# Where the sums of squares are formed: GpSimd or VectorE, and when TensorE takes them up

## The chip, the cores and the metric

The kernel runs on one core of a Trainium2 chip. The metric is the time on the device in microseconds. Three runs of the kernel before gave 1308.89, 1309.41 and 1309.84 us, median 1309.41.

## The reference

Two decoder layers work on a stream x of 512 tokens by 1024 features, all in f32. Layer 0 mixes tokens by an RWKV-7 recurrence, layer 1 by dilated attention; both also attend to 256 memory tokens, and both end in a gated MLP with a causal convolution of width 3. The change is about three of the RMS norms:

```python
def rmsnorm(x, g):
    xf = f32(x)
    return xf * lax.rsqrt(jnp.mean(xf * xf, axis=-1, keepdims=True) + RMS_EPS) * f32(g)
# layer i:  h = rmsnorm(x, attn_norm[i]); ... x = x + y @ w_out
#           x = x + conv_ffn(x, ...)   where conv_ffn starts with rmsnorm(x, g) @ w_up
```

## The kernel before, in words

The stream is kept with features on the 128 partitions: x is eight slices (KD = 8) of 128 by 512 tokens. Every matrix product is made of three products of rounded parts: a weight tile is split into w_hi, a copy that ScalarE rounds, and w_lo, the difference that VectorE forms (L2118) or GpSimd (L3036); the stream's slices likewise into in_hi and in_lo, or b_hi and b_lo. Weight tiles come by DMA into a ring of four slots. w_hi and w_lo have two buffers, so ScalarE can round tile n once TensorE is through with tile n-2.

Each engine runs a program written out by hand, in order; semaphores tie them together. A norm is not applied before the product. TensorE multiplies the raw stream; meanwhile the sum over the features of x squared is formed, and the result of the product is scaled when VectorE reads it (L2548). For the sum, ScalarE squares each slice of x into y (L1793 before an MLP, L1843 for layer 1), GpSimd adds the slices y[1] to y[6] to y[0], one after the other, each add waiting for the one before it (sum_squares, L3008, L3014), and TensorE multiplies by a matrix of ones.

The four places of the change:

1. MLP start (square_sum, L1161, called in mlp ahead of the second of the first two up-projection tiles). TensorE makes two products of ones, with y[0], the sum, and with y[7], into bank 7. The rows of the trace call them "bank<-y,cst 128x512"; each f32 product is two passes. Then ScalarE takes the root (stream_root, L1515), VectorE the reciprocal (stream_rstd, L2111), and VectorE reads the first tile's product. In VectorE's order the low part of the fourth tile stands behind that read and the one after it, and in ScalarE's order the high part of the fourth tile behind own_tap of the first. A tile is eight k-steps of three matmuls (split_product, L675).

2. The down-projection of the first MLP's second half runs in four rounds o, each of two slices of x. The weights of a round come as seven blocks (A11, A12, A22, S2, S4, S1, S3), each rounded by ScalarE (block_high) and VectorE (block_low). Behind its blocks of a round ScalarE does stream_high(m), which makes b_hi[m] and y[m] from the finished slice m of x: m = 2o after the next round's A22, and m = 2o + 1 at the end of the round. GpSimd adds the squares as they come.

3. Layer 1's projections, 20 tiles s. In tile s TensorE runs over four groups r of tokens and two k-steps b, and at slot 2r + b it calls between(s, slot). token_sums (L1247) is called at tile 1, slot 4: products of y[0] and y[7] with two columns of ones ("bank<-cst,y 128x2"), which give the sums by token. VectorE's order here: stream_low(0) to (7), that is b_lo, then rope_tables, then in tile 1 token_rms (L2662), which waits for the sums. GpSimd forms w_lo of tile s + 2.

4. Second MLP: residual (L2399) on VectorE and squares (L1784) on ScalarE go through the eight slices of x; GpSimd adds; square_sum as in 1.

Of the kernel before, what the change touches and what calls it, by code (L numbers as in the profile page):

```python
# [145 lines left out]
def trunk(nc, xT, memT, consts, params, ropes, masks, w_small, w_mem, w_pairs, w_ring, outT):  # L146
    ctx = ExitStack()
    with ctx:
# [242 lines left out]
        def part_count(stage, o, i):  # L391

            if o == 0:
                at = 1 if i is None else i + 2
            else:
                at = 5 if i is None else 6 if i == S4 else i + 1
            return 2 * PAIRS + 1 + 6 * (4 * stage + o) + at

        def parts_used(stage, o, i):
            return 3 * (N_OUTA + 3 * PAIRS) + 7 * (4 * stage + o) + i + 1  # L400
# [262 lines left out]
        def _(pe):  # L663
# [496 lines left out]

            def square_sum(q):  # L1161

                pe.wait_ge(sem("sq_sum"), (KD - 2) * (q + 1))
                mm(bank[7][:, :], ones, y[:, 0, :], True, False)
                pe.wait_ge(sem("xsq"), KD * (q + 2))
                mm(bank[7][:, :], ones, y[:, KD - 1, :], False, True).then_inc(sem("x_ss"), 1)

            def mlp(l, h_at):
                for half in range(2):
                    up, down = mlp_tiles(l, half)  # L1170
                    g0 = FT * l + HALF * half
                    e, stage = 3 * l + 1 + half, 2 * l + half

                    def up_pair(p, q, j):
                        if not isinstance(p, int) or g0 + p >= 2:
                            pe.wait_ge(sem("up_read"), 2 * p + 2 * (g0 - 1))
                        for s in range(2):
                            if half == 0 and q == 0 and s == 1:
                                square_sum(2 * l)
                            if half == 1 and q == 0 and s == 1:  # L1180
                                pe.wait_ge(sem("x_up"), KD * e)
                            n = up + 2 * q + s
                            split_ready(2 * p + (up + s))
                            b = 2 * ((g0 + q) % 2) + s
                            split_product(bank[b][:, :], n, in_hi, in_lo, KD,
                                          ready=("h_ready", h_at + 1) if q == 0 and s == 0 and half == 0 else None)\
                                .then_inc(used, 1)

                    mlp_pairs(pe, up_pair)

                    def product(o, i, out, adds=False):

                        part = MOVING[i]
                        if i < S1:
                            pe.wait_ge(sem("part_lo"), part_count(stage, o, i))
                        else:
                            split_ready(down + 2 * o + i - S1)
                        hi, lo = block_slot(w_hi_all, o, i), block_slot(w_lo_all, o, i)
                        for j in range(ZP):
                            ks = slice(j * P, (j + 1) * P)  # L1200
                            at = slice(PARTW * j + TH * part, PARTW * j + TH * (part + 1))
                            mm(out, hi[:, ks], z[:, 0, at], j == 0 and not adds, False)
                            mm(out, hi[:, ks], z[:, 1, at], False, False)
                            q = mm(out, lo[:, ks], z[:, 0, at], False, j == ZP - 1)
                        return q

                    def plain(o, s, ks=range(ZC)):

                        out = bank[down_banks(g0, o)[s]][:, :]
                        pe.wait_ge(sem("part_lo"), part_count(stage, o, None))  # L1210
                        for k in ks:
                            p = (0, HALF - 2, HALF - 1)[k]
                            if o == 0:
                                pe.wait_ge(sem("z"), z_count(stage, p))
                            cs = slice(k * P, (k + 1) * P)
                            first = k == 0 and o == 0
                            mm(out, plain_slot(w_hi_all)[:, s, cs], z_plain(0, p), first, False)
                            mm(out, plain_slot(w_hi_all)[:, s, cs], z_plain(1, p), False, False)
                            q = mm(out, plain_slot(w_lo_all)[:, s, cs], z_plain(0, p), False, k == ZC - 1)
                        return q  # L1220

                    pe.wait_ge(sem("z"), z_count(stage, 2, ZP - 1, 2))
                    for o in range(4):
                        a, b, c = (bank[i] for i in down_banks(g0, o))
                        low, high = slice(0, TH), slice(TH, T)
                        pe.wait_ge(sem("x_up"), KD * e + 2 * (o - 1) if o > 1 else KD * e)
                        if o == 1:
                            pe.wait_ge(sem("up_read"), 2 * (g0 + HALF))
                        if o == 0:
                            plain(o, 0, (0, 1))  # L1230
                            plain(o, 1, (0,))
                        product(o, A11, c[:, low]).then_inc(sem("part_used"), 1)
                        product(o, A12, a[:, low], o == 0).then_inc(sem("part_used"), 1)
                        product(o, A22, b[:, low], o == 0).then_inc(sem("part_used"), 1)
                        pe.wait_ge(sem("accumulated"), added(stage, o, 1))
                        product(o, S2, c[:, low], True).then_inc(sem("part_used"), 1)
                        product(o, S4, a[:, high], True).then_inc(sem("part_used"), 1)
                        plain(o, 0, range(2 if o == 0 else 0, ZC)).then_inc(used, 1)
                        pe.wait_ge(sem("accumulated"), added(stage, o, 2))
                        product(o, S1, c[:, low]).then_inc(sem("part_used"), 1)  # L1240
                        plain(o, 1, range(1 if o == 0 else 0, ZC)).then_inc(sem("part_used"), 1)
                        pe.wait_ge(sem("x_up"), KD * e + 2 * o + 1)
                        product(o, S3, c[:, low]).then_inc(used, 1)
# [2 lines left out]

            def token_sums():  # L1247

                pe.wait_ge(sem("sq_sum"), 2 * (KD - 2))
                pe.wait_ge(sem("xsq"), 3 * KD)  # L1250
                for r in range(RES):
                    for m in (0, KD - 1):
                        q = mm(bank[7][:, 2 * r:2 * r + 2], residues(y[:, m, :])[:, r, :], ones[:, 0:2], m == 0, m > 0)
                q.then_inc(sem("x_ss"), 1)
# [74 lines left out]

            def between(s, slot):  # L1330

                if (s, slot) == (1, 4):
                    token_sums()
                if slot == 1 and 5 <= s <= 16:
                    turn_heads(s - 5)
# [123 lines left out]
        def _(act):  # L1459
# [343 lines left out]
            def mlp(l):  # L1803
                for half in range(2):
# [86 lines left out]
                    for o in range(4):  # L1891
                        if o:
                            block_high(o, S4)
                        block_high(o, S1)
                        block_high(o, S3)
                        if o < 3:
                            block_high(o + 1, A11)
                            block_high(o + 1, A12)
                            block_high(o + 1, A22)
                            stream_high(2 * o)  # L1900
                            block_high(o + 1, S2)
                            plain_high(o + 1)
                            stream_high(2 * o + 1)
                    split(down + KD)
                    stream_high(KD - 2)
                    split(down + KD + 1)
# [11 lines left out]
                copy(w_hi[:, n % 2, 0:w], ring[:, i, 0:w]).then_inc(sem("w_hi"), 1)  # L1918

            mlp(0)  # L1920
            act.wait_ge(sem("sq_sum"), 2 * (KD - 2))

            def group_done(g, r):

# [78 lines left out]
            for s in range(GROUPS * PARTS + 1):  # L2003
# [2 lines left out]
                    squares_out(g - 1, RES - 1)  # L2006
                if 0 < s < GROUPS * PARTS:
                    split(N_PROJ + s + 1)
                if s == 1:
                    act.wait_ge(sem("x_eps"), 2)  # L2010
                    root(tok_rstd, bank[7][:, 0:8], D, rms_eps).then_inc(sem("x_sd"), 1)
                if s in KV_AT:
# [89 lines left out]
        def _(dve):  # L2102
# [698 lines left out]
            def operand_low(i):  # L2801
# [2 lines left out]
                dve.wait_ge(sem("in_hi"), 5 * KD + 1 + i + 1)  # L2804
                lower(out_b_operand(k)[1], y[:, k, :], out_b_operand(k)[0], "y_split")

            rope_tables()
            for s in range(GROUPS * PARTS):
                g = s // PARTS
                if s == 1:  # L2810
                    token_rms()
                if s in (3, 7, 11):
                    rope_parts(g, 0)
# [88 lines left out]
            operand_low(2)  # L2902
            operand_low(3)
            residual(N_OUTB, 3, 0.5)
            mlp(1, 0)


        @block.gpsimd
        def _(pool):
# [95 lines left out]
                pool.wait_ge(sem("q_high"), Q0 + 12 * PAIRS + i + 1)  # L3005
                G.tensor_tensor(out_low[k], y[:, k, :], out_high[k].bitcast(F32), ALU.subtract).then_inc(sem("y_split"), 1)

            def sum_squares(q):  # L3008

                for m in range(1, KD - 1):  # L3010
                    pool.wait_ge(sem("xsq"), KD * (q + 1) + m + 1)
                    if m > 1:
                        pool.wait_ge(sem("sq_sum"), (KD - 2) * q + m - 1)
                    G.tensor_tensor(y[:, 0, :], y[:, 0, :], y[:, m, :], ALU.add).then_inc(sem("sq_sum"), 1)  # L3014

            sum_squares(0)
            sum_squares(1)
            pool.wait_ge(sem("w_lo"), N_PROJ + 2 - N_SPLIT)
            def head_scaled(e):

# [20 lines left out]
                    for e in range(2 * s - 18, 2 * s - 16):  # L3041
                        head_scaled(e)

            sum_squares(2)

# [124 lines left out]
```

## Time and profile before

| what | value |
|---|---|
| median of three runs | 1309.41 us |
| profiled execution | 1308.9 us |
| its span | 1307.0 us |
| TensorE busy | 1275.2 us, 98% |
| VectorE busy | 992.2 us, 76% |
| ScalarE busy | 646.0 us, 49% |
| GpSimd busy | 321.3 us, 25% |
| granted TensorE clock, mean | 1.000 |

The span is the time from the first to the last instruction of the profiled execution; the execution's own time is 1.9 us longer. Busy shares are of the span. A row of a timeline gives the start from the beginning of the span, the length, engine, line and operation, the tiles written and read, the shape, and in brackets for how long the engine sat idle before it and what released it. Neighbouring instructions of one kind are merged into one row with their count.

### The profile page before, as it was taken

The page shows a single profiled execution, that of the slowest core. Times are in us where ns is not written, and L with a number is a line of the kernel's source. Part 1 is how long each engine was busy: PE and PEld are TensorE (multiplying, and loading weights), DVE is VectorE, ACT ScalarE, POOL GpSimd, SP SyncE. Part 2 cuts the span into 40 slices and gives each one's busy share as a digit, 9 for nine tenths or more (in the row PEclk, how much of TensorE's full clock was granted, in tenths as well). Part 3 has the DMA queues.
Part 4 walks back from the last instruction along what each step waited for, and adds up shares of the span by engine and source line. Part 5 has one row for each costly group of instructions (what it writes and reads, how often), then busy time and mean ns, then how long its engine had stood idle before and what let it go on. Part 6 is the DMA issues. An engine that isn't in the chain of part 4 may idle for free.

```text
span 1307.0 us, 27113 instructions
## 1 busy us (share of the span) xinstructions
PE 1275.2 (98%) x10688; PEld 1041.3 (80%) x10688; DVE 992.2 (76%) x1486; ACT 646.0 (49%) x1068; POOL 321.3 (25%) x302
## 2 busy tenths in 40 slices
PE   7999999999999999999999999999999999999999
PEld 5876777776578888988889988776778889888898
DVE  4777777787468889857889958548578899578896
ACT  6575645563244445334546555547554453344542
POOL 3369777784420000000001256330100000000000
PEclk9999999999999999999999999999999999999999
DMA  8100111114023332233332342211133323333331
GB/s 326 49 22 32 55 55 40 55 32 168 18 97 97 96 108 90 86 104 96 96 105 90 112 143 81 65 49 33 33 98 97 96 89 122 97 96 98 119 109 46
DMA packets 30055, 114.35 MB, mean 87 GB/s; under 512 B 3456, under 2 KB 5248, under 8 KB 29184
## 3 DMA queue, kind: packets, MB, share of 16 engines
q1 hardware_dynamic: 29952, 112.89, 26.0%
q8 instruction: 76, 1.25, 0.4%
q14 instruction: 27, 0.22, 0.1%
HBM read 110.78 MB, written 2.10 MB: 86 GB/s over the span
## 4 chain that ended last, share of the span: by engine, by line
PE 86%; DVE 5%; ACT 3%; issue 1%; POOL 0%; DVEq 0%; POOLq 0%; ACTq 0%
PE bank L665 84%; PE bank L1384 1%; DVE arena L2132 1%; ACT arena L1581 1%; PE bank L971 0%; DVE sin_part L2696 0%; DVE cos_part L2723 0%; DVE in_lo L2143 0%; PE bank L1266 0%; DVE head_stat L2706 0%; ACT w_hi L1464 0%; DVE w_lo L2118 0%; PE bank L1289 0%; DVE stat L2210 0%; DVE cos_part L2692 0%
## 5 line engine op out<-in xcount | busy, mean ns | idle before, releaser
L665 PE MATMUL bank<-in_hi,w_hi 128*128 128x512 f32 x704 | 274.9, 390 | 0.9 <-DVE in_lo L2143 0.9
L665 PE MATMUL bank<-in_lo,w_hi 128*128 128x512 f32 x704 | 273.9, 389 | 0.0
L665 PE MATMUL bank<-in_hi,w_lo 128*128 128x512 f32 x704 | 273.9, 389 | 0.0
L1464 ACT ACTIVATE w_hi<-ring 128x1024 fp32r<-128x1024 f32 (+2 forms) x176 | 161.4, 919 | 205.2 <-PE bank L665 204.9
L665 PE MATMUL bank<-z,w_hi 128*128 128x256 f32 (+1 forms) x1088 | 221.9, 303 | 0.7 <-DVE w_lo L2118 0.7
L665 PEld LDWEIGHTS bank<-z,w_hi 128*128 128x128 f32 x1088 | 175.9, 191 | 9.7 <-DVE w_lo L2118 0.9
L2118 DVE TENSOR_TENSOR w_lo<-ring,w_hi 128x1024 fp32r<-128x1024 f32 (+2 forms) x156 | 161.1, 1035 | 26.4 <-ACT w_hi L1464 25.0
L665 PE MATMUL bank<-z,w_lo 128*128 128x256 f32 (+1 forms) x544 | 164.1, 302 | 0.0
L665 PEld LDWEIGHTS bank<-in_hi,w_hi 128*128 128x128 f32 x704 | 132.2, 188 | 29.6 <-DVE in_lo L2143 1.3
L665 PEld LDWEIGHTS bank<-in_lo,w_hi 128*128 128x128 f32 x704 | 132.2, 188 | 27.7 <-issue 0.5
L665 PEld LDWEIGHTS bank<-in_hi,w_lo 128*128 128x128 f32 x704 | 132.1, 188 | 27.4
L665 PEld LDWEIGHTS bank<-arena 64*64 64x64 f32 (+2 forms) x4064 | 109.1, 136 | 50.0 <-issue 37.3
L2556 DVE SCALAR_TENSOR_TENSOR conv<-up_raw,par,conv 128x511 f32<-128x511 f32 (+1 forms) x176 | 131.8, 749 | 17.4 <-DVE conv L2556 9.8
L665 PE MATMUL bank<-arena 64*64 64x64 f32 (+4 forms) x4064 | 132.3, 239 | 7.1 <-DVE arena L2185 1.7
L3014 POOL TENSOR_TENSOR y<-y 128x512 f32<-128x512 f32 x18 | 24.7, 1371 | 425.8 <-ACT y L1843 352.1
L665 PEld LDWEIGHTS bank<-z,w_lo 128*128 128x128 f32 x544 | 103.8, 191 | 4.0
L1853 ACT ACTIVATE conv<-up_raw,par 128x512 f32<-128x512 f32 x88 | 71.3, 810 | 43.6 <-DVE up_raw L2548 43.2
L2548 DVE TENSOR_TENSOR up_raw<-bank,rstd 128x512 f32<-128x512 f32 x88 | 60.5, 687 | 34.8 <-PE bank L665 34.6
L1464 ACT ACTIVATE arena<-bank 128x512 f32<-128x512 f32 (+1 forms) x72 | 40.8, 584 | 65.0 <-PE bank L665 52.6
L1464 ACT ACTIVATE z<-z_raw 128x256 f32 (+2 forms) x44 | 24.4, 555 | 97.2 <-DVE z_raw L2569 97.2
L3036 POOL TENSOR_TENSOR w_lo<-ring,w_hi 128x1024 fp32r<-128x1024 f32 x20 | 48.7, 2434 | 80.6 <-ACT w_hi L1464 80.6
L665 PE MATMUL bank<-w_hi,b_hi 128*128 128x512 f32 x160 | 66.2, 414 | 0.0
(292 smaller groups left out, 2239.3 us busy)
## 6 DMA issues: line engine op xcount, KB each, us to landing
ring<-w_ring SPq DMA_DIRECT2D x119, 512.0 KB, 3.5
ring<-w_ring SPq DMA_DIRECT2D x32, 704.0 KB, 4.1
ring<-w_pairs SPq DMA_DIRECT2D x18, 512.0 KB, 3.9
arena<-w_mem SPq DMA_DIRECT2D x2, 2048.0 KB, 19.0
arena<-w_ring SPq DMA_DIRECT2D x4, 512.0 KB, 4.9
x<-xT SPq DMA_DIRECT2D x1, 2048.0 KB, 8.5
outT<-x SPq DMA_DIRECT2D x8, 256.0 KB, 2.0
mask<-masks SPq DMA_DIRECT2D x1, 1536.0 KB, 7.0
```

Of the source, the lines that this page charges most:

```text
L665: return nc.tensor.matmul(out, lhsT, rhs, start=first, stop=last, skip_group_check=True)
L1384: m = nc.tensor.transpose(psum[:, 4:7, :].rearrange("p b t -> p (b t)")[:, at:at + P], sm[n % 3][:, b, q * P:(q + 1) * P], ident)
L1464: return nc.scalar.activation(out, in_, ACT.Copy)
L1581: nc.scalar.activation(mem_slots(l, c)[:, k, :], bank[b + hh][:, i * NMEM:(i + 1) * NMEM], ACT.Exp, bias=stat[:, 4 + k:5 + k], scale=mem_s ...
L1853: nc.scalar.activation(conv[:, 2 * b + s, :], up_raw[:, 2 * b + s, :], ACT.Identity, scale=tap(l, tile, 2), bias=tap(l, tile, 3)).then_inc ...
L2118: V.tensor_tensor(dst, src, high.bitcast(F32), ALU.subtract).then_inc(sem(sig), 1)
L2132: V.reciprocal(rs, rs).then_inc(sem("hn_rc"), 1)
L2548: V.tensor_tensor(up_raw[:, 2 * b + s, :], bank[2 * b + s][:, :], rstd[:, :], ALU.mult).then_inc(sem("up_read"), 1)
L2556: V.scalar_tensor_tensor(out=c[:, lag:T], in0=u[:, 0:T - lag], scalar=tap(l, 2 * p + (2 * HALF * half + s), 2 - lag), in1=c[:, lag:T], op0 ...
L3014: G.tensor_tensor(y[:, 0, :], y[:, 0, :], y[:, m, :], ALU.add).then_inc(sem("sq_sum"), 1)
L3036: G.tensor_tensor(w_lo[:, n % 2, 0:w], ring[:, n % SLOTS, 0:w], w_hi[:, n % 2, 0:w].bitcast(F32), ALU.subtract).then_inc(sem("w_lo"), 1)
```

## The change

A function squares_summed(q, n) gives the count of the semaphore sq_sum after n adds of norm q (q = 0 first MLP, 1 layer 1, 2 second MLP). In both MLPs y[7] is added as well, so there are seven adds and one product of ones; it is made inside the second up-projection tile, before k-step 2 in the first MLP and before k-step 6 in the second. The adds of layer 1 (six) and of the second MLP (seven) are on VectorE: the six behind stream_low and ahead of rope_tables, the seven between residual and mlp(1, 0). On ScalarE stream_high of the odd slices stands behind the next round's S4, S1 and S3, and its wait for sq_sum after the first MLP is gone. token_sums is called at tile 2, slot 4, and the root and token_rms of it in tile 2.

```diff
+        def squares_summed(q, n):
+            return (0, KD - 1, 2 * KD - 3)[q] + n
...
             def square_sum(q):
-                pe.wait_ge(sem("sq_sum"), (KD - 2) * (q + 1))
-                mm(bank[7][:, :], ones, y[:, 0, :], True, False)
-                pe.wait_ge(sem("xsq"), KD * (q + 2))
-                mm(bank[7][:, :], ones, y[:, KD - 1, :], False, True).then_inc(sem("x_ss"), 1)
+                pe.wait_ge(sem("sq_sum"), squares_summed(q, KD - 1))
+                mm(bank[7][:, :], ones, y[:, 0, :]).then_inc(sem("x_ss"), 1)
...
-                            if half == 0 and q == 0 and s == 1:
-                                square_sum(2 * l)
+                            sum_at = (2, KD - 2)[l] if half == 0 and q == 0 and s == 1 else None
...
                             split_product(bank[b][:, :], n, in_hi, in_lo, KD,
+                                          between=lambda k: square_sum(2 * l) if k == sum_at else None,
...
             def token_sums():
-                pe.wait_ge(sem("sq_sum"), 2 * (KD - 2))
+                pe.wait_ge(sem("sq_sum"), squares_summed(1, KD - 2))
                 pe.wait_ge(sem("xsq"), 3 * KD)
...
-                if (s, slot) == (1, 4):
+                if (s, slot) == (2, 4):
                     token_sums()
...
                         block_high(o, S1)
                         block_high(o, S3)
+                        if o:
+                            stream_high(2 * o - 1)
...
                             plain_high(o + 1)
-                            stream_high(2 * o + 1)
...
             mlp(0)
-            act.wait_ge(sem("sq_sum"), 2 * (KD - 2))
...
-                if s == 1:
+                if s == 2:
                     act.wait_ge(sem("x_eps"), 2)
                     root(tok_rstd, bank[7][:, 0:8], D, rms_eps).then_inc(sem("x_sd"), 1)
...
+            for m in range(1, KD - 1):
+                dve.wait_ge(sem("xsq"), 2 * KD + m + 1)
+                if m > 1:
+                    dve.wait_ge(sem("sq_sum"), squares_summed(1, m - 1))
+                V.tensor_tensor(y[:, 0, :], y[:, 0, :], y[:, m, :], ALU.add).then_inc(sem("sq_sum"), 1)
             rope_tables()
             for s in range(GROUPS * PARTS):
-                if s == 1:
+                if s == 2:
                     token_rms()
...
             residual(N_OUTB, 3, 0.5)
+            for m in range(1, KD):
+                dve.wait_ge(sem("xsq"), 3 * KD + m + 1)
+                if m > 1:
+                    dve.wait_ge(sem("sq_sum"), squares_summed(2, m - 1))
+                V.tensor_tensor(y[:, 0, :], y[:, 0, :], y[:, m, :], ALU.add).then_inc(sem("sq_sum"), 1)
             mlp(1, 0)
...
-            def sum_squares(q):
-                for m in range(1, KD - 1):
+            def sum_squares(q, last):
+                for m in range(1, last + 1):
...
-            sum_squares(0)
-            sum_squares(1)
+            sum_squares(0, KD - 1)
...
-            sum_squares(2)
```

## Rows read from the trace of the kernel before

**Rows 1.** The page, part 1: busy us, share of span, instructions
```profile
PE 1275.2 (98%) x10688; PEld 1041.3 (80%) x10688; DVE 992.2 (76%) x1486; ACT 646.0 (49%) x1068; POOL 321.3 (25%) x302
```

**Rows 2.** TensorE's waits: for what, us in total, times, longest
```profile
PE bank L665 <- DVE in_lo L2143: 0.9, 1, 0.9
PE bank L665 <- DVE w_lo L2118: 0.9, 2, 0.7
```

**Rows 3.** Timeline of TensorE at the first MLP's product of ones
```profile
389.95 1.88 PE L665 MATMUL bank<-y,cst 128*128 128x512 f32 x4
...
391.90 0.40 PE L665 MATMUL bank<-in_lo,w_hi 128*128 128x512 f32 x1
```

**Rows 4.** Timelines of ScalarE and VectorE behind it
```profile
391.87 0.69 ACT L1461 ACTIVATE rstd<-bank,epsb 128x512 f32<-128x512 f32 x1 [0.60 <-PE bank L665]
...
399.61 1.21 DVE L2118 TENSOR_TENSOR w_lo<-ring,w_hi 128x1024 fp32r<-128x1024 f32 x1
```

**Rows 5.** Timeline of TensorE in the down-projection, round o = 1
```profile
702.52 0.28 PE L665 MATMUL bank<-z,w_lo 128*128 128x256 f32 x1
703.52 0.50 PE L665 MATMUL bank<-z,w_hi 128*128 128x256 f32 x2 [0.72 <-DVE w_lo L2118]
```

**Rows 6.** Timelines of ScalarE, VectorE and GpSimd at that gap
```profile
700.42 1.12 ACT L1843 ACTIVATE y<-x 128x512 f32<-128x512 f32 x1
...
702.10 1.37 DVE L2118 TENSOR_TENSOR w_lo<-up_raw,w_hi 128x512 fp32r<-128x512 f32 x1 [1.05 <-ACT w_hi L1464]
...
701.62 1.30 POOL L3014 TENSOR_TENSOR y<-y 128x512 f32<-128x512 f32 x1 [318.88 <-ACT y L1843]
```

**Rows 7.** VectorE at layer 1's start: instructions of L2143, then one of the timeline
```profile
L2143 DVE SCALAR_TENSOR_TENSOR b_lo<-x,par,b_hi x8: 1122/1137/3148, 734.1 to 747.9; 128x512 fp32r<-128x512 f32 x8
...
750.99 1.42 DVE L2675 TENSOR_TENSOR rope_tab<-roped 128x256 f32<-128x256 f32 x4
```

**Rows 8.** Timeline of GpSimd: its first two w_lo of layer 1
```profile
747.64 2.57 POOL L3036 TENSOR_TENSOR w_lo<-ring,w_hi 128x1024 fp32r<-128x1024 f32 x1 [4.89 <-ACT w_hi L1464]
754.83 2.42 POOL L3036 TENSOR_TENSOR w_lo<-ring,w_hi 128x1024 fp32r<-128x1024 f32 x1 [4.62 <-ACT w_hi L1464]
```

**Rows 9.** Timeline of VectorE: a chained pair, then one not chained
```profile
720.38 0.68 DVE L2473 TENSOR_TENSOR t_raw<-ring 128x512 f32<-128x512 f32 x1
721.19 0.69 DVE L2473 TENSOR_TENSOR t_raw<-t_raw,ring 128x512 f32<-128x512 f32 x1
721.79 0.69 DVE L2118 TENSOR_TENSOR w_lo<-ring,w_hi 128x512 fp32r<-128x512 f32 x1
```

**Rows 10.** Timeline of TensorE: start of tile 1, and the token sums
```profile
746.15 0.39 PE L665 MATMUL bank<-w_hi,b_hi 128*128 128x512 f32 x1
...
748.88 1.84 PE L665 MATMUL bank<-cst,y 128*128 128x2 f32 x16
```

**Rows 11.** Instructions of L2723 (ns min/median/max, 792 to 822), GpSimd beside the longest
```profile
L2723 DVE TENSOR_TENSOR cos_part<-cos_part,sin_part x8: 626/1105/2889, 792.1 to 819.2; 128x512 f32<-128x512 f32 x8
...
819.07 2.43 POOL L3036 TENSOR_TENSOR w_lo<-ring,w_hi 128x1024 fp32r<-128x1024 f32 x1 [0.34 <-ACT w_hi L1464]
```

**Rows 12.** Timelines of GpSimd and VectorE before the second MLP
```profile
940.95 1.43 POOL L3014 TENSOR_TENSOR y<-y 128x512 f32<-128x512 f32 x1 [0.81 <-ACT y L1793]
...
941.15 1.77 DVE L2143 SCALAR_TENSOR_TENSOR in_lo<-x,par,in_hi 128x512 fp32r<-128x512 f32 x1
...
953.22 1.22 DVE L2118 TENSOR_TENSOR w_lo<-ring,w_hi 128x1024 fp32r<-128x1024 f32 x1
```

**Rows 13.** Timelines of TensorE and VectorE at the second MLP's start
```profile
947.41 0.47 PE L665 MATMUL bank<-in_hi,w_hi 128*128 128x512 f32 x1
...
954.17 1.88 PE L665 MATMUL bank<-y,cst 128*128 128x512 f32 x4
...
957.52 3.35 DVE L2113 RECIPROCAL rstd<-rstd 128x512 f32<-128x512 f32 x1 [0.78 <-ACT rstd L1461]
...
964.54 1.21 DVE L2118 TENSOR_TENSOR w_lo<-ring,w_hi 128x1024 fp32r<-128x1024 f32 x1
```

More of the change, by code:

```diff
@@ L3006, in _ @@
                 G.tensor_tensor(out_low[k], y[:, k, :], out_high[k].bitcast(F32), ALU.subtract).then_inc(sem("y_split"), 1)
-            def sum_squares(q):
-                for m in range(1, KD - 1):
+            def sum_squares(q, last):
+                for m in range(1, last + 1):
                     pool.wait_ge(sem("xsq"), KD * (q + 1) + m + 1)
                     if m > 1:
-                        pool.wait_ge(sem("sq_sum"), (KD - 2) * q + m - 1)
+                        pool.wait_ge(sem("sq_sum"), squares_summed(q, m - 1))
                     G.tensor_tensor(y[:, 0, :], y[:, 0, :], y[:, m, :], ALU.add).then_inc(sem("sq_sum"), 1)
-            sum_squares(0)
-            sum_squares(1)
+            sum_squares(0, KD - 1)
             pool.wait_ge(sem("w_lo"), N_PROJ + 2 - N_SPLIT)
```

## The prediction

> **What bounds the kernel now.** I read the page's first part first: TensorE is busy for 98% of the span [rows 1]. The time can move in two ways only, by work taken off TensorE or by its waits, so the second view is TensorE's list of waits. The two rows that the edits can reach are 0.9 us behind VectorE's in_lo and 0.9 us in two waits behind VectorE's w_lo [rows 2]. VectorE, ScalarE and GpSimd matter only where TensorE comes to wait for them. The third view is therefore the timelines around the four places that are edited: the start of each MLP, the last down-projection of the first MLP, and the first four projection tiles of layer 1. All positions below are in microseconds of the span of before. The profiled execution took 1308.9 us (span 1307.0), the median of the runs is 1309.41, 0.5 more; I sum against 1308.9 and add the 0.5 at the end.
>
> **1. First MLP: one ones-product in place of two.** The two products are four passes on TensorE, which start at 389.95. The product behind them has its second matmul at 391.90, and in it a matmul follows every 0.23 us [rows 3], so without them the second would be at 389.95 + 0.23 = 390.18. The pair costs 1.72 us, a pass 0.43, one product 0.86. Gain 0.86 us.
> The product also moves by two k-steps (six matmuls, 6 x 0.2275 = 1.37 us), to 389.95 + 1.37 = 391.32. It waits for seven GpSimd adds now; an add takes 1.30 to 1.43 us [rows 6, 12], its square is ready near 387, and it is done by about 389.7 even if it has to let a VectorE operation through. No wait. What is late next is the chain behind the product: Sqrt on ScalarE, reciprocal, the first read, ScalarE's tap and w_hi, and then VectorE's low part of the weights of the fourth tile (L2118). In the trace Sqrt starts at 391.87, which is 1.92 after the first pass, and the low part starts 7.74 later and takes 1.21 [rows 4]: 10.87 from the first pass. With two passes fewer it is 10.87 - 0.86 = 10.0. TensorE has 0.86 for the product, six k-steps (4.10) and one tile (8 x 3 x 0.2275 = 5.46) until it needs that part: 10.42. It fits by 0.4 us; if the cover were gone it would cost what is missing of it, up to some 0.5.
>
> **2. Last down-projection of the first MLP.** ScalarE no longer does stream_high(2o+1) ahead of the three high parts S4, S1, S3, and GpSimd no longer adds squares here. TensorE's gap is between 702.52 and 703.52, where 0.12 is normal [rows 5]: 0.88 us lost. Before it stands ScalarE, in y at 700.42 and not at the S4 high part before 701.45, and VectorE's low part from 702.10 takes 1.37 where 0.68 is usual, beside a GpSimd add from 701.62 [rows 6]. In the new order the S4 high part comes at about 698.4, and VectorE does the low part as soon as it has done its stream add of 700.63, by about 701.7. TensorE needs it at 702.64. The 0.88 us go. The other two rounds have no such gap, and gain nothing. The high parts pushed behind (stream_high(1), (3), (5)) are wanted by layer 1 after 740 only.
>
> **3. Token sums: six adds on VectorE, one tile later.** The sums now stand behind VectorE's last five b_lo, so they begin where rope_tab began, at 750.99 [rows 7]. The fifth b_lo took 3.15 in place of 1.14, because GpSimd's low part of a weight tile ran from 747.64 to 750.2 [rows 7, 8]; VectorE was held while it ran. A VectorE queue that is some 0.35 us earlier (a GpSimd add beside its w_lo is gone) meets the same GpSimd operation and ends at the same time, whichever of the two goes first. Each add waits for the one before it. Where an add waits so, the next starts 0.81 later, where it does not, 0.60 later [rows 9]. Six adds end 5 x 0.81 + 0.68 = 4.73 later, at 755.7.
> TensorE reaches the new place earlier than before, since the sums (1.8 us) have left the second tile: that tile starts at 746.15 [rows 10], ends 5.46 later at 751.61, and half a tile on (2.73) TensorE is at the sums, at 754.34. So it waits at least 1.4 us. And with the second tile over at 751.6, ScalarE makes the next w_hi by about 752.96 (1.06 long) and GpSimd starts its low part near 753.05 (before: 754.83 [rows 8]), in the middle of the adds. What such an operation does to a VectorE add of two SBUF tiles is seen at 819: beside a GpSimd w_lo of 2.43 an add took 2.89, where the shortest took 0.63 and an unhindered one takes some 0.66 [rows 11]: 2.2 more. The adds end at about 757.9, and TensorE loses 757.9 + 0.05 - 754.34 = 3.6 us. Bounds: 1.4 (no hold) and 4.2 (both holds in full and a loose pitch); I take 3.6, as both rows that show the pairing have the hold. Queued behind the waiting product on TensorE is everything; nothing later gives it back, since VectorE and ScalarE are fed by TensorE from here. rope_tables, the norm and tok_rstd come some 7 us later, and are wanted from the fourth tile's end (762 and later): hidden. The dropped ScalarE wait was met long before, 0.
> What the Trainium skill says on this is weighed here. SBUF — State Buffer, section "Who interferes with whom", has a VectorE operation with two SBUF inputs blocked for the whole of a GpSimd instruction that came first; that would be the 2.4 of the operation itself and not 2.2, and the sum 0.2 us higher. VectorE: DVE Perf Modes, section "The DRAIN you can't avoid", holds that a semaphore between VectorE operations costs nothing extra; the rows have 0.81 against 0.60, so they speak against it for chained adds.
>
> **4. Second MLP: seven adds on VectorE, product at k = 6.** First what is gained. In the residual stage four VectorE operations ran beside GpSimd adds: in_lo at 941.15 took 1.77 beside the add of 940.95 [rows 12], where 0.75 is usual, another such at 947.24, and two w_lo of 1.52 against 1.22. That is 2 x 1.02 + 2 x 0.30 = 2.64 us. VectorE has no wait of its own in the stretch that would eat them (I replayed it with ScalarE's high parts in between), so w_lo of the second tile, 953.22 to 954.44 [rows 12], ends at 951.8. TensorE's first tile, which started 0.15 late at 947.41 and then waited 0.9 for in_lo [rows 2], runs from 947.26 to 952.72; the next begins there, in place of 954.17 [rows 13].
> The adds start at 951.7 and end 6 x 0.81 + 0.68 = 5.54 later, at 957.25. TensorE is at k = 6 at 952.72 + 4.10 = 956.82 and waits 0.5, the product starts at 957.3. Sqrt follows 1.06 behind (1.92 - 0.86; its table is loaded by then, which was on the chain before), the reciprocal 0.72 after that, at 959.1. In the trace the fourth tile's low part ends 964.54 + 1.21 - 957.52 = 8.23 after the reciprocal's start [rows 13], so now at 967.3. TensorE wants it at 957.3 + 0.86 + 1.37 + 5.46 = 965.0: a new wait of 2.3 us. The fourth tile starts at 967.4; before it was 954.17 + 1.72 + 2 x 5.46 = 966.8. Net loss 0.6 us: 1.45 and 0.86 are gained, 0.5 and 2.4 are lost. Bounds: 0.1 if the adds follow at 0.60, 1.8 if the fifth tile comes late too. I take 0.6.
>
> **Sum.** -0.86 - 0.88 + 3.6 + 0.6 = +2.5 us. 1308.9 + 2.5 = 1311.4 for a profiled execution, 1311.9 for the median. From the bounds of steps 3 and 4 the forecast's own range is 1309.3 to 1313.9, mostly 1310.6 to 1313.
>
> **Rivals.**
> A, other side: TensorE never waits at the token sums. It decides at 754.34: if VectorE's sixth add is over by then, step 3 costs nothing, the sum is -1.74 + 0.6 = -1.1, and the median 1308.3. For it: without both holds the adds would run from 748.65 to 753.4. Against it: the 3.15 of the last b_lo, and that the queue in front of it starts from ScalarE's w_hi at 742.2, which TensorE's progress sets.
> B: only the first hold counts, the second GpSimd operation falls behind the adds. The wait is 1.4, the sum +0.3, the median 1309.7. The row at 819 speaks against it.
> C: chained adds follow at 0.60. Then six end at 754.7 without a hold, at 756.9 with one, the wait is 2.6 and step 4 costs 0.1: +1.0, median 1310.4. This is what the Trainium skill's VectorE page would give by its DRAIN section; the three pairs of rows at 0.81 leave it little.
> D: step 4 goes on. The low part of the fifth tile ended at 971.3 and was wanted at 972.2, a reserve of 0.9, and everything on VectorE comes 1.6 later there; if it and the one after it are late as well, or step 1's 0.4 us does not hold, 1 to 2 us more: 1313.9.
>
> **Chances.** Forecast 0.55, A 0.15, B 0.12, C 0.08, D 0.10. About what can be told from no change is 0.2%, 2.6 us: above 1312.0 or below 1306.8. Above lie nearly half of the forecast (0.26) and D (0.10): 0.36. Below lies only what would come of A with no loss in step 4 either (-3.6 at best, if the new wait there is absent as well): 0.07. Between them 0.57. The range 1307.8 to 1313.4 leaves out the deep end of A and most of D.
>
> **What would show it.** Right: the product's row of the sums holds two passes at about 391.3 and 0.86 less; the gap at 702.5 is gone; a TensorE wait of 3 to 4 us for VectorE's y ahead of the 128x2 products; in the second MLP no wait for in_lo, a short wait for y and one of over 2 us for w_lo. GpSimd's w_lo lies inside the chain of adds, and one add is over 2 us long. Wrong: no wait ahead of the 128x2 products (A), one of 1.4 (B), adds at 0.60 (C), a wait of over 1 us in the first MLP.

## The result and the profile after

The changed kernel took 1314.36 us (median of 6 runs, 1312.39 to 1317.16), the kernel before 1309.62 beside it (1308.78 to 1310.22). The ratio is 1.0039, 95% interval 1.0028 to 1.0050: slower by 4.7 us. The forecast was 1311.9, range 1307.8 to 1313.4. The direction was right, the time 2.5 us too low and outside the range.

The profiled execution took 1312.84 us, span 1311.1, which is 4.1 more than the span of before. Part 1 of its page answers [rows 1]; the columns are the same.

```profile
PE 1276.1 (97%) x10684; PEld 1042.1 (79%) x10684; DVE 996.8 (76%) x1499; ACT 646.4 (49%) x1068; POOL 310.3 (24%) x291
```

TensorE has four instructions fewer and 0.9 us more busy time. GpSimd has lost the eleven instructions that the change takes from it. TensorE's waits, against [rows 2]: in_lo is gone, and there are two large new ones.

```profile
PE bank L668 <- DVE y L2812: 3.1, 1, 3.1
PE bank L668 <- DVE w_lo L2119: 2.4, 2, 2.2
PE bank L668 <- DVE y L2915: 0.3, 1, 0.3
```

First MLP, TensorE and ScalarE [rows 3, 4]: one product, two passes, at 391.67, and the root that waits for it. Nothing waits at the fourth tile.

```profile
391.67 1.02 PE L668 MATMUL bank<-y,cst 128*128 128x512 f32 x2
...
392.76 0.39 PE L668 MATMUL bank<-in_lo,w_hi 128*128 128x512 f32 x1
...
392.73 0.69 ACT L1462 ACTIVATE rstd<-bank,epsb 128x512 f32<-128x512 f32 x1 [1.11 <-PE bank L668]
```

The down-projection, TensorE [rows 5]: matmuls follow each other by 0.12 and 0.24 through 703, with no idle time in brackets.

```profile
702.38 0.28 PE L668 MATMUL bank<-z,w_lo 128*128 128x256 f32 x1
702.50 0.40 PE L668 MATMUL bank<-z,w_hi 128*128 128x256 f32 x2
...
703.58 0.63 PE L668 MATMUL bank<-z,w_hi 128*128 128x512 f32 x2
```

The token sums: VectorE, GpSimd, then TensorE [rows 7, 8, 10]. The six adds take 8.94 us, where six chained ones without a hold would take 5 x 0.81 + 0.68 = 4.73; the first of GpSimd's two w_lo is still running when they begin, the second falls in their middle. The median add takes 0.69, the longest 2.86, and the fourth, beside the second w_lo, 2.79. TensorE waits 3.09 and then does the 128x2 products. Look at the two lengths behind them: 0.63 with starts 0.43 apart, where the same matmul is otherwise 0.39 and 0.23 apart.

```profile
746.87 8.94 DVE L2812 TENSOR_TENSOR y<-y 128x512 f32<-128x512 f32 x6
...
L2812 DVE TENSOR_TENSOR y<-y x6: 692/693/2857, 746.9 to 755.1; 128x512 f32<-128x512 f32 x6
...
755.72 1.43 DVE L2676 TENSOR_TENSOR rope_tab<-roped 128x256 f32<-128x256 f32 x4
...
745.91 3.26 POOL L3046 TENSOR_TENSOR w_lo<-ring,w_hi 128x1024 fp32r<-128x1024 f32 x1 [357.19 <-ACT w_hi L1465]
751.29 2.38 POOL L3046 TENSOR_TENSOR w_lo<-ring,w_hi 128x1024 fp32r<-128x1024 f32 x1 [2.12 <-ACT w_hi L1465]
...
755.86 2.02 PE L668 MATMUL bank<-cst,y 128*128 128x2 f32 x16 [3.09 <-DVE y L2812]
757.74 0.78 PE L668 MATMUL bank<-w_hi,b_hi 128*128 128x512 f32 x1
758.31 0.63 PE L668 MATMUL bank<-w_hi,b_lo 128*128 128x512 f32 x1
758.74 0.63 PE L668 MATMUL bank<-w_lo,b_hi 128*128 128x512 f32 x1
```

The same place in stretches of 2 us. The columns are the stretch, its length, the busy time of PE, PEld, DVE, ACT and POOL (with the count of instructions), the granted clock of TensorE, the DMA share and GB/s.

```profile
754.00:756.00 2.00, 0.14 (x2) 0.14 (x2) 1.79 (x4) 0.00 (x0) 0.00 (x0) 1.00 0.58 176
756.00:758.00 2.00, 2.00 (x17) 2.00 (x18) 1.23 (x5) 0.00 (x0) 0.00 (x0) 0.90 0.21 86
758.00:760.00 2.00, 2.00 (x5) 1.54 (x6) 0.28 (x2) 0.27 (x1) 0.00 (x0) 0.50 0.00 0
760.00:762.00 2.00, 2.00 (x8) 1.61 (x7) 0.00 (x0) 0.00 (x0) 0.00 (x0) 0.75 0.00 0
762.00:764.00 2.00, 2.00 (x11) 1.62 (x10) 0.00 (x0) 1.38 (x3) 0.50 (x1) 1.00 0.00 0
```

After some 5 us in which TensorE had next to nothing to do (the wait and then products of two columns, 752.6 to 757.7) the granted clock is at 0.50, the lower of its two levels (1.2 of 2.4 GHz), until about 761. The rows give its length: 0.4 us in the second stretch, 2.0 in the third and 1.0 in the fourth, 3.4 together. A busy share doesn't show it: TensorE is 2.00 of 2.00 busy there, with 5 matmuls in place of 11.

The second MLP, VectorE and TensorE [rows 12, 13]. The seven adds take 5.46, a pitch of (5.46 - 0.68) / 6 = 0.80. One product waits 0.27 for them, and the fourth tile 2.20 for its w_lo.

```profile
953.83 1.22 DVE L2119 TENSOR_TENSOR w_lo<-ring,w_hi 128x1024 fp32r<-128x1024 f32 x1
954.97 5.46 DVE L2915 TENSOR_TENSOR y<-y 128x512 f32<-128x512 f32 x7
...
969.38 1.22 DVE L2119 TENSOR_TENSOR w_lo<-ring,w_hi 128x1024 fp32r<-128x1024 f32 x1
...
950.53 0.39 PE L668 MATMUL bank<-in_hi,w_hi 128*128 128x512 f32 x1
...
960.48 1.12 PE L668 MATMUL bank<-y,cst 128*128 128x512 f32 x2 [0.27 <-DVE y L2915]
...
970.65 0.50 PE L668 MATMUL bank<-in_hi,w_hi 128*128 128x512 f32 x1 [2.20 <-DVE w_lo L2119]
```

TensorE's clock differs from run to run. The six runs of the changed kernel had a mean granted clock of 0.999 to 0.995, and the time follows it roughly: 1312.39 (0.998) and 1312.84 (0.999) at one end, 1315.79 (0.996) and 1317.16 (0.995) at the other. Of the 95 runs of the kernel before that were made beside the experiments below, 94 had 1.000 and one 0.999 (1311.16 us, its slowest).

### The profile page after: what moved, and what is told of

Same layout as the page of the kernel before. It is cut to its first block, busy times and chain, and to the rows that moved or that the text cites. A ratio compares the mean times of both kernels' runs of the same rounds, so it can differ in the third digit from the quotient of the medians.

```text
span 1311.1 us, 27109 instructions
## 1 busy us (share of the span) xinstructions
PE 1276.1 (97%) x10684; PEld 1042.1 (79%) x10684; DVE 996.8 (76%) x1499; ACT 646.4 (49%) x1068; POOL 310.3 (24%) x291
## 4 chain that ended last, share of the span: by engine, by line
PE 83%; DVE 7%; ACT 3%; issue 1%; POOL 0%; DVEq 0%; POOLq 0%; ACTq 0%
PE bank L668 82%; DVE y L2812 1%; PE bank L1385 1%; DVE arena L2133 1%; ACT arena L1582 1%; DVE w_lo L2119 0%; PE bank L974 0%; DVE b_lo L2144 0%; DVE sin_part L2697 0%; DVE cos_part L2724 0%; PE bank L1267 0%; ACT w_hi L1465 0%; DVE head_stat L2707 0%; DVE y L2915 0%; PE bank L1290 0%
## 5 line engine op out<-in xcount | busy, mean ns | idle before, releaser
L668 PE MATMUL bank<-w_hi,b_lo 128*128 128x512 f32 x160 | 63.1, 395 | 0.0
```

Source lines behind the costliest of these rows:

```text
L668: return nc.tensor.matmul(out, lhsT, rhs, start=first, stop=last, skip_group_check=True)
```

## The experiments

After the result my theory T was: step 3's wait stands where the forecast put it, and what is missing in the sum is TensorE's clock, which falls after a stretch of little work on TensorE. Its rivals stand in the expectations. All kernels ran in five rounds; the ratio is to the kernel before on the same chip, whose median was 1309.2 to 1309.4 each time.

**The parts alone.** First only the first MLP's product, the rest as before:

```diff
-  mm(bank[7], ones, y[0], True, False); mm(bank[7], ones, y[7], False, True)   # first MLP
+  mm(bank[7], ones, y[0])     # GpSimd adds y[7] as well
```

> The kernel before with the first MLP's part alone: seven adds on GpSimd, one product ahead of k = 2. Both theories: 0.86 us faster, 1308.7, clock 1.000, no new wait at the fourth tile. A wait there would cost up to 0.5.

1308.83 us (ratio 0.9993, 0.9984 to 1.0002), the clock 1.000 in all 11 runs, no new wait. As forecast within what can be told.

Only layer 1: sums on VectorE, ScalarE's order, the token sums in tile 2; both MLPs with two products and GpSimd's adds.

> The kernel before with the layer-1 part alone (ScalarE's new order, six adds on VectorE, token sums at tile 2, slot 4); both MLPs keep two products of ones and GpSimd's adds. Theory T: TensorE waits 3.1 us for the adds, as in the changed kernel, and its clock then falls to 1.2 GHz for some microseconds. The gap of 0.88 us in the down-projection goes, so +3.3 - 0.9 = +2.4 by the wait, and 1.5 to 6 more by the clock: 1313 to 1318 us, with a mean granted clock under 1.000 in every run and the time rising as it falls. Rival R (the loss lies in the second MLP, or is spread): +0 to +2.5, clock 1.000 in all runs.

1314.62 us (1.0040, 1.0026 to 1.0054), clock 0.999 to 0.996 in its five runs. This part alone costs as much as the whole change. In its profile the clock had fallen before the products began and stayed low for 6.8 us, so that they took 3.58 in place of 1.84. TensorE's row, and two stretches:

```profile
756.56 3.58 PE L668 MATMUL bank<-cst,y 128*128 128x2 f32 x16 [2.93 <-DVE y L2823]
...
756.00:758.00 2.00, 1.44 (x7) 1.44 (x7) 1.85 (x5) 0.00 (x0) 0.00 (x0) 0.53 0.48 195
...
760.00:762.00 2.00, 2.00 (x6) 1.61 (x7) 0.37 (x2) 0.27 (x1) 0.00 (x0) 0.50 0.00 0
```

Only the second MLP: seven adds on VectorE, one product at k = 6.

> The kernel before with the second MLP's part alone: seven adds on VectorE, one product ahead of k = 6. Theory T: waits of 0.3 us for the adds and 2.2 for the fourth tile's w_lo, 0.6 to 0.8 us slower than before: 1310.3; no fall of the clock, since the profile of the changed kernel shows none behind that wait of 2.2 us. Rival R: this part carries the missing time too, 2 us or more and a clock under 1.000.

1310.23 us (1.0009, 1.0000 to 1.0018). Seven of 11 runs had the clock at 1.000 (1309.21 to 1310.86), four at 0.999 or 0.998 (1310.90 to 1312.48). Its profile has the waits of the whole change, 0.27 and 2.21. The forecast of the time held; T's forecast that the clock would not fall here missed. The profiled execution is one of the seven, so it doesn't show where the four fell; the wait of 2.21 is the only long stretch of little work that is new in it.

The changed kernel with layer 1's sums back on GpSimd and the token sums back in tile 1; ScalarE's new order stays:

```diff
-  for m in range(1, KD - 1): V.tensor_tensor(y[0], y[0], y[m], add)    # ahead of rope_tables
+  sum_squares(1, KD - 2)                                               # GpSimd
-  if (s, slot) == (2, 4):
+  if (s, slot) == (1, 4):
       token_sums()
```

> The changed kernel with the layer-1 sums alone put back: six adds on GpSimd, token sums at tile 1, slot 4. ScalarE's new order and both MLP parts stay. Theory T: the 3.1 us wait and its fall of the clock go, and the gap of 0.88 us in the down-projection stays away: 1309.4 - 0.86 - 0.88 + 0.85 = 1308.5, with a clock of 0.998 to 0.999 in a third of the runs, as in e2. If the gap there was GpSimd's doing and not ScalarE's order, it comes back: 1309.4.

1310.23 us (1.0005, 0.9996 to 1.0014), 4.1 below the changed kernel's median, but 1.7 above T's forecast of 1308.5, which had the clock fall in a third of the runs. The four runs at clock 1.000 took 1308.18 to 1309.20, the seven at 0.999 or 0.998 took 1310.21 to 1310.99. The gap of [rows 5] is gone here as well, with GpSimd's adds back: it was ScalarE's order that closed it. Two smaller ones have come further on, though. The starts of the first matmuls at 709.33 and 724.08 are 0.53 and 0.68 behind the matmul before, where 0.23 is normal, 0.75 us lost together, and VectorE's w_lo at 704.07 and 718.83 take 1.37 in place of 0.69 beside GpSimd's adds. The changed kernel, without those adds, has neither. So the order closes the old gap, and most of the gain is kept only with the adds gone from GpSimd as well.

```profile
708.80 0.39 PE L668 MATMUL bank<-z,w_lo 128*128 128x512 f32 x1
709.33 0.51 PE L668 MATMUL bank<-z,w_hi 128*128 128x256 f32 x2
...
723.40 0.39 PE L668 MATMUL bank<-z,w_lo 128*128 128x512 f32 x1
724.08 0.51 PE L668 MATMUL bank<-z,w_hi 128*128 128x256 f32 x2 [0.29 <-DVE x L2496]
```

**Wait or clock.** TensorE's wait filled with matmuls whose result nobody reads (their bank is overwritten by the sums). In the changed kernel, 13 of them, which leave little of the wait:

```diff
 def token_sums():
+    for _ in range(13):
+        mm(bank[7], b_hi[0][:, 0:128], w_hi[tile 2])
```

> The changed kernel with 13 useless products of 128x512 (0.2275 us each, 2.96 us) into bank 7 ahead of the wait for the token sums; the sums overwrite them. TensorE's work grows by 2.96 us and its wait shrinks from 3.1 to about 0.2; the order of everything else stays. Theory T: the extra time was the clock's fall behind the idle wait, so 1311.4 us, 3 us faster than the changed kernel's median, clock 1.000 in all runs and little spread. Rival R (clock unrelated to the wait): no change, 1314.4, the same spread from 1312.4 to 1317.2.

1312.81 us (1.0022, 1.0013 to 1.0031). The forecast of T missed. Four of 11 runs had clock 1.000 and took 1310.60 to 1311.90, as T said; four had 0.999, three 0.997 (1314.18 to 1314.95). The profile shows the clock falling still, 1.3 us behind the 128x2 products, which now follow full work. It falls a second time in the second MLP, behind the wait of 2.21 there, so not every run below 1.000 need have fallen at the sums:

```profile
756.43 1.95 PE L668 MATMUL bank<-cst,y 128*128 128x2 f32 x16 [0.18 <-DVE y L2814]
...
759.48 0.48 PE L668 MATMUL bank<-w_lo,b_hi 128*128 128x512 f32 x1
759.76 0.63 PE L668 MATMUL bank<-w_hi,b_hi 128*128 128x512 f32 x1
...
972.00:974.00 2.00, 2.00 (x6) 1.52 (x6) 1.30 (x2) 1.23 (x3) 0.00 (x0) 0.50 0.73 250
```

The idle wait is therefore not all: products of two columns, busy by the page, belong to the stretch of little work. The next kernel takes the wait away whole: the layer-1 part alone, with 20 fillers, more than the wait was long.

> The kernel of e1 (layer-1 part alone) with 20 useless products of 128x512 ahead of the token sums, 4.55 us of dense work in place of the 2.9 us wait: TensorE never waits there, and the stretch of little work is only the sums' own 1.8 us, as in the kernel before. Theory T, sharpened after e3 (the clock falls behind a stretch of waiting and 128x2 products together when it is longer than the 1.8 us that the kernel before has; e3 still had 2.1): clock 1.000 in all runs, 1311.8 + 1.6 = 1313.4 us with a spread of some 2 us. Rival P (the fall belongs to the place or to the 128x2 products, not to the wait): clock under 1.000 in most runs, 1315 us or more.

1312.66 us (1.0028, 1.0017 to 1.0038), clock 1.000 in all 8 runs, within 1.1 us of each other. It does 20 x 0.2275 = 4.55 us more on TensorE than the first layer-1 kernel, its sums come 1.6 us later (758.14 against 756.56), and it is 2.0 us faster by the medians (on two chips; the intervals of the two ratios overlap, so the times lean this way and the clocks, low in 5 of 5 runs against 0 of 8, decide). The profile has the products at their old length and the clock at 1.00 behind them.

```profile
758.14 1.84 PE L668 MATMUL bank<-cst,y 128*128 128x2 f32 x16
...
760.00:762.00 2.00, 2.00 (x9) 1.62 (x10) 0.37 (x2) 0.27 (x1) 0.00 (x0) 1.00 0.00 0
```

Here T holds and rival P falls: delay and clock are two prices, and this pair tells them apart by the clock.

**Where the sums stand.** The changed kernel with the token sums at slot 6 of tile 2, a quarter of a tile later, and then at the start of tile 3:

```diff
-  if (s, slot) == (2, 4):
+  if (s, slot) == (2, 6):      # the other kernel: (3, 0), with the root and token_rms in tile 3
       token_sums()
```

> The changed kernel with the token sums a quarter of a tile later, tile 2, slot 6: TensorE arrives 1.36 us later and waits 1.7 us in place of 3.1. Theory T: between e7 (wait 0.4) and the changed kernel; 1.4 us of wait go, and the stretch of waiting and 128x2 products shrinks from 5.1 to 3.7 us, so the clock still falls in most runs: 1311 to 1313, clock 0.997 to 1.000. Rival R (no link of clock and wait): 1313, the spread as in the changed kernel.

1312.73 us (1.0027, 1.0015 to 1.0038). The wait is 1.40, and all 7 runs had a clock of 0.998 to 0.996. The time fits T and the rival R alike (1311 to 1313, and 1313). The profiled execution, at a mean of 0.997, has two falls of 3.4 us, one at 758.5 behind the sums and one at 970.1 behind the wait of 2.21 in the second MLP.

> The changed kernel with the token sums (and their root and reciprocal) half a tile later, at the start of tile 3. The adds end at the same time, TensorE arrives 2.73 us later and waits 0.4 in place of 3.1. Theory T: 2.7 us of wait and most of the clock's loss go: 1309.5 to 1310 with a clock of 0.999 in some runs. Rival R (clock unrelated to the wait): 1311.7, the spread as in the changed kernel.

1309.22 us (0.9999, 0.9990 to 1.0008), 5.1 below the changed kernel for half a tile's delay of the sums, and 0.3 better than T's 1309.5 to 1310. R had 1311.7. Seven of 11 runs had 1.000 (1307.96 to 1309.39), four 0.999 (1309.71 to 1310.24). The profiled run is one of the four. Its clock stays 1.00 behind the sums and falls at the second MLP, after the 2.20 of idle time:

```profile
756.03 1.92 PE L668 MATMUL bank<-cst,y 128*128 128x2 f32 x16 [0.28 <-issue]
...
966.00:968.00 2.00, 1.53 (x6) 1.24 (x7) 1.83 (x3) 1.97 (x3) 0.00 (x0) 0.98 0.20 45
968.00:970.00 2.00, 2.00 (x6) 1.61 (x5) 1.19 (x2) 1.24 (x3) 0.00 (x0) 0.50 0.57 217
970.00:972.00 2.00, 2.00 (x7) 1.56 (x7) 1.93 (x3) 1.23 (x2) 0.00 (x0) 0.67 0.00 0
```

**The second MLP's wait.** Three kernels. Seven adds on GpSimd and the product at k = 2, with layer 1 as in the kernel with its sums back:

> ScalarE's new order and the first MLP's part as changed; layer-1 sums on GpSimd at tile 1, slot 4; second MLP: seven adds on GpSimd and one product ahead of k = 2. No wait of over 0.9 us is left that the kernel before has not: -0.86 - 0.88 and in the second MLP -0.86 + 0.3 for w_lo of the second tile: 1307.2 us, clock 1.000 in all runs. If GpSimd's adds hold VectorE as before, the gap in the down-projection stays: 1308.0.

1309.20 us (1.0002, 0.9993 to 1.0011), forecast missed. TensorE's wait of 0.90 for in_lo in the kernel before is still there (0.93), and two microseconds on a new one of 1.24 follows, for w_lo of the second tile: GpSimd's last add is at work when VectorE comes to it. Four runs were at 0.999; the profiled one isn't among them. Next, the second MLP alone on VectorE, with ScalarE's and VectorE's work on the fourth tile's weights ahead of the tap and the read:

```diff
+  split_at(p, up + 3, q)       # ScalarE: right behind stream_root
   own_tap(0)
-  split_at(p, up + 3, q)
+  split(up + 3)                # VectorE: right behind read(0)
```

> The kernel of e2 (second MLP's part alone) with the fourth tile's weights formed first: in the first pair of each MLP ScalarE makes its w_hi right behind the root, ahead of own_tap, and VectorE its w_lo right behind the first read. Theory T: that w_lo is ready some 1.7 us before TensorE wants it, the 2.2 us wait is gone and with it the clock's occasional fall: 1309.3 + 0.85 - 2.35 = 1307.8, clock 1.000 in all runs. If the wait had another cause, 1310.2 as e2.

1312.31 us (1.0021, 1.0012 to 1.0030), worse than without it (1310.23); the forecast was 1307.8. The edit reaches both MLPs, and the first one's fifth tile now waits 0.28. In the second the fourth tile no longer waits, the fifth does, for 2.45, and the clock falls behind it:

```profile
974.25 0.50 PE L668 MATMUL bank<-in_hi,w_hi 128*128 128x512 f32 x1 [2.45 <-DVE w_lo L2133]
...
975.43 0.63 PE L668 MATMUL bank<-in_lo,w_hi 128*128 128x512 f32 x1
```

The order within the queue hands the wait on; VectorE's adds and its reciprocal of 3.35 stay ahead of all of it. The same edit with the sums in tile 3:

> The changed kernel with the token sums at the start of tile 3 (as e7) and the fourth tile's weights first (as e9). Both new waits of the change are gone but for 0.3 to 0.4 us at either place: 1309.2 - 2.3 = 1306.9 at the clock of e7's better runs, 1306.3 by the sum of the parts (-0.86 - 0.88 + 0.4 - 1.7), clock 1.000 in all runs; 0.2% faster than the kernel before.

1310.62 us (1.0013, 1.0004 to 1.0022), where 1306.9 was forecast: the same wait, 2.44, and eight of 11 runs below 1.000. Last, the sums in tile 3 and the second MLP as before:

> The changed kernel with its token sums at the start of tile 3 instead of the middle of tile 2, and with the second MLP as before (six GpSimd adds and two ones-products); the rest of the change stays. Theory T (TensorE's granted clock falls only after a stretch of little work, and the 2.2 us wait in the second MLP is the last such stretch of the kernel that had its sums in tile 3): no wait of over 1 us is left, the granted clock is 1.000 in every run, and the time is that of before less 0.86 (one product in the first MLP) and 0.88 (the gap in the down-projection), with up to 0.4 back in small waits: 1307.5 to 1308.2, I say 1307.9. Rival S (sums on VectorE in tile 3 themselves cost time or clock): runs below 1.000 remain and the median stays at 1309.2. Rival Q (the projection stream pays the two gains back in other waits): clock 1.000 in all runs, but the median is 1309 or above.

1308.55 us (0.9994, 0.9985 to 1.0003), the lowest median of all, though the interval still takes in no change and the first MLP's part alone has the same ratio (0.9993). The six runs at 1.000 took 1307.54 to 1308.55; the forecast had 1307.5 to 1308.2 for all. But five runs had 0.999 and took 1309.10 to 1309.52, which T had excluded, and the profiled one fell behind the sums, with 2.2 us of little work (755.22 to 757.43) ahead of it:

```profile
755.65 1.92 PE L668 MATMUL bank<-cst,y 128*128 128x2 f32 x16 [0.28 <-issue]
757.43 0.49 PE L668 MATMUL bank<-w_hi,b_hi 128*128 128x512 f32 x1
...
758.00:760.00 2.00, 2.00 (x7) 1.61 (x6) 0.20 (x1) 0.58 (x3) 1.12 (x1) 0.62 0.00 0
```

So rival S is right in its first half (runs below 1.000 remain). Its second half, that the median stays at 1309.2, isn't settled: this one is 0.7 lower, but on another chip and with intervals that overlap.

## Why the prediction was wrong

**Step 1, right.** The pair became one product of two passes at 391.67, forecast 391.3, and nothing waits behind it. The part alone gave 0.6 by the medians, 0.9 by the ratio, neither of them clear of no change; in the trace it is 392.76 - 391.67 - 0.23 = 0.86, as forecast.

**Step 2, right.** The gap is gone. The argument named two causes, ScalarE's order and GpSimd's add. The kernel with layer 1's sums back shows that the order alone closes this gap, and that with GpSimd's adds still there two others open, of 0.75 us together; so taking the adds off GpSimd is needed as well to keep the 0.88.

**Step 3, right in its wait, wrong in its sum.** This is the step that failed: "TensorE loses 757.9 + 0.05 - 754.34 = 3.6 us". TensorE was ready at 752.38 + 0.23 = 752.61, which is the 754.34 less the 1.74 of steps 1 and 2. The products came at 755.86: 3.25 lost, inside the step's bounds of 1.4 and 4.2. Both holds by GpSimd are there, and rivals A and B are out. The first falls on the first add and not on the last b_lo; the step had allowed for that. The step then let TensorE go on as if nothing had happened. In the profiled execution, seven matmuls between 757.74 and 760.87 start up to 0.57 apart, mostly 0.43, in place of 0.23: 3.13 - 7 x 0.2275 = 1.5 us, with some 0.3 more in the products ahead of them and the matmul behind. The whole part cost 5.0 there: the second MLP's first tile starts 3.12 later than before (947.41 to 950.53), 3.27 with the late start of 0.15 that is gone, and the first two steps had brought 1.74, so 3.27 + 1.74 = 5.0 was lost between. Taking the 3.25 away leaves 1.8 for the clock, and half the clock for 3.4 us takes 3.4 / 2 = 1.7 us of work. The slowest run of the changed kernel took some 4 us more. Its runs without a profile give only the mean clock. Its two middle ones (1314.34 and 1314.38) had 0.997, and the three profiled executions of other kernels at that mean show what can lie behind it: with 13 fillers and with slot 6 two such falls, at the sums and in the second MLP, with the layer-1 part alone one of twice the length. The changed kernel's profile has a single fall of 3.4.

**Step 4, right.** VectorE's operations before the adds are back at 0.75 and 1.22, the in_lo wait is gone, the adds follow by 0.80, the product waits 0.27 (forecast 0.5), the fourth tile 2.20 (2.3). It starts at 970.65; less the 3.27 that it inherits, at 967.38, where the forecast had 967.4. What was not seen is that an idle stretch of 2.2 us there can also bring the clock down: in the profiles of the kernels with 13 fillers, with slot 6 and with the sums in tile 3, and most likely in the four of 11 runs of this part alone.

**The rivals.** C, adds at 0.60, is out: 0.80 in the seven. The Trainium skill, VectorE: DVE Perf Modes, section "The DRAIN you can't avoid", measured eight copies with and without semaphores between them and found that these cost nothing extra. For adds that wait for each other the rows disagree, with 0.80 against 0.60. D is out too: the second short wait for w_lo, 0.19 at 939.51, is that of the kernel before (0.17 at 936.23), and nothing behind the fourth tile waits for w_lo. None of the rivals had the clock in it. The sum with every wait as measured is 1308.9 - 1.74 + 3.25 + 0.57 = 1311.0 for a profiled execution, where the forecast had 1311.4. Of the 1.9 us from there to 1312.84, 1.8 are the missing term as the rows of step 3 show it. From the profiled execution to the median it is 1.5 more, where the forecast had allowed 0.5 from the runs of before: that is most likely the same term, as the mean clock of the other runs is lower. The range left it out too. (The forecast's own range was also added up slightly wrong: its bounds give 1309.2 to 1313.7, not 1309.3 to 1313.9. The time lies outside both.)

**What is shown and what is open.** Shown: the granted clock falls behind the stretches of little work that the change makes, and where such a stretch is filled, it doesn't. By length, with the runs below 1.000 out of all:

| stretch of little work | length | runs below 1.000 |
|---|---|---|
| sums with no wait: before; first MLP's part alone; layer-1 part with 20 fillers | 1.7 us | 1 of 95; 0 of 11; 0 of 8 |
| a wait in the second MLP, alone; with layer 1 back | 2.2 us | 4 of 11; 7 of 11 |
| the same at the fifth tile (weights first) | 2.4 us | 8 of 11 |
| two waits in the second MLP, 0.93 and 1.24 (adds on GpSimd) | 3.3 us, with three matmuls in it | 4 of 11 |
| sums at the start of tile 3: alone; and the 2.2 wait; and the 2.4 wait | 2.2 us | 5 of 11; 4 of 11; 8 of 11 |
| sums with 13 fillers (and the 2.2 wait) | 2.1 us | 7 of 11 |
| sums at slot 6 of tile 2 (and the 2.2 wait) | 3.2 us | 7 of 7 |
| the changed kernel (and the 2.2 wait); layer-1 part alone | 5 us | 6 of 6; 5 of 5 |

Open: what decides in a single run. Executions of one kernel differ, the one low run of the kernel before included (it was not profiled, so where its clock fell isn't known), and length is not all: two stretches of 2.2 us brought no more low runs (4 of 11) than one (5 of 11). Early in the kernel before, in the recurrence, TensorE waits 1.66 and 1.15 us with small products between, and the mean clock is 1.000 in 94 of 95 runs:

```profile
106.91 1.10 PE L665 MATMUL bank<-arena 64*64 64x128 f32 x32 [1.66 <-DVE arena L2185]
...
110.18 1.10 PE L665 MATMUL bank<-arena 64*64 64x128 f32 x32 [1.15 <-DVE arena L2382]
```

The place of the falls in runs without a profile isn't known; the runs give only the mean clock.

## What to carry to other kernels

Where TensorE has been dense, a new wait of a few microseconds has two prices: its length, and the clock that it may take away afterwards, here 1.8 us in the profiled execution and more in others. Look at the granted clock in short stretches behind each new wait, and behind a run of products of very few columns too, which the busy share shows as full work. A chain of adds moved to the engine that also makes the next operands must be placed with what is queued behind it: here taking up the sums half a tile later was worth 5 us, and changing the order within the queue only handed the wait to the next tile.

## What the hardware showed that I had not expected

The granted clock fell after 2 to 5 us of little work in a kernel that is otherwise 97% busy, stayed at 0.50 for 3.4 us (6.8 in one profile), and came back by itself; in the same kernel it fell in one run and not in the next. The Trainium skill, TensorE: Matmul & The Clock Gate, Part 1, has the two levels; the rows of 0.43 and 0.23 agree with them. A GpSimd w_lo that met VectorE already at work ran 3.26 us instead of 2.4, and 3.93 in the last kernel, so the holding seems to go both ways; no run tests this. VectorE's adds with two inputs in SBUF lost 8.94 - 4.73 = 4.2 us to two such operations. The Trainium skill, SBUF — State Buffer, section "Who interferes with whom", has such a VectorE instruction contend with a GpSimd instruction that reads SBUF. The trace agrees, with adds of 2.86 and 2.79 in place of 0.69.
